# Handing over by token tile between the stages of a two-block network on one core

## The reference, cut to what matters

```python
# first block, layers i = 0, 1
h  = h + mixers(rms_norm(h, g_mix[i]) @ w_in[i]) @ w_out[i]
hn = rms_norm(h, g_ffn[i])
h  = h + (swiglu(hn) if i == 0 else moe_swiglu(hn))     # 8 experts, each token takes 2
gate = sigmoid(rms_norm(h, g_ple[i]) @ ple_gate_w[i])
h  = h + (p[i] @ ple_proj_w[i]) * gate                   # the "embedding part"
x  = rms_norm(h, g_final)
# second block, layers l = 0, 1; sh, sc, g come from silu(c) @ ada_w[l] + ada_b[l]
x = x + g1 * (mixers2((rmsnorm(x, g) * (1 + sc1) + sh1) @ w_in[l]) @ w_out[l])
x = x + g2 * swiglu(rmsnorm(x, g) * (1 + sc2) + sh2)
return rmsnorm(x, final_g)
```

## Time and profile before

| | |
|---|---|
| time of 3 runs, median (lowest to highest) | 2287.8 us (2281.92 to 2294.17) |
| the profiled execution: its time | 2287.38 us |
| its span from first to last instruction | 2286.0 us |
| PE busy | 2176.0 us, 95% of the span |
| DVE busy, ACT busy | 696.2 us (30%), 421.6 us (18%) |
| mean granted clock of TensorE | 0.974 of full |
| read from memory | 520.39 MB |

### The profile page before, as it was taken

One profiled execution on the slowest core, in us unless ns is written; L12 is line 12 of the kernel. 1 busy time (PEld: TensorE's weight loads), 2 busy tenths in 40 slices (PEclk: granted clock), 3 DMA queues, 4 the chain that ended last, 5 costly groups with the idle time before them and its releaser, 6 DMA issues.

```text
span 2286.0 us, 28880 instructions
## 1 busy us (share of the span) xinstructions
PE 2176.0 (95%) x12233; PEld 1270.5 (56%) x12233; DVE 696.2 (30%) x1453; ACT 421.6 (18%) x952; POOL 0.2 (0%) x4
## 2 busy tenths in 40 slices
PE   8988999989979999999999999889999999989998
PEld 5664777765755533333323232365677776657775
DVE  2563375223662100100111001125436533730001
ACT  2464000022462000000000000132310002320001
POOL 0000000000000000000000000000000000000000
PEclk9998999999979999999999999999999999999999
DMA  5222987023301999899999999422199532247400
GB/s 220 89 100 87 423 324 285 26 99 131 109 32 74 426 409 391 331 375 425 393 419 403 396 425 393 171 79 106 56 402 373 218 150 82 76 166 303 152 24 19
DMA packets 55143, 523.38 MB, mean 229 GB/s; under 512 B 6368, under 2 KB 6880, under 8 KB 16864
## 3 DMA queue, kind: packets, MB, share of 16 engines
q1 hardware_dynamic: 45792, 471.13, 51.0%
q10 hardware_dynamic: 9216, 50.34, 5.9%
HBM read 520.39 MB, written 1.05 MB: 228 GB/s over the span
## 4 chain that ended last, share of the span: by engine, by line
PE 87%; DVE 7%; ACT 4%; issue 1%; DMA 1%; DVEq 0%; SPq 0%; ACTq 0%
PE ps L89 87%; DVE ring L89 5%; ACT ring L89 2%; DVE stat L89 1%; DVE natural L89 1%; DVE residual L89 0%; ACT transposed L89 0%; ACT L89 0%; DMA ring<-in_moe 0%; DVE transposed L89 0%; DMA constants<-in_const 0%; ACT natural L89 0%; ACT stat L89 0%; DVE gates L89 0%; ACT z L89 0%
## 5 line engine op out<-in xcount | busy, mean ns | idle before, releaser
L89 PE MATMUL ps<-ring 128*32 128x512 f32 (+10 forms) x3812 | 536.6, 515 | 10.0 <-ACT ring L89 3.7
L89 PE MATMUL ps<-ring,transposed 128*128 128x384 f32 (+4 forms) x1408 | 475.7, 495 | 3.6 <-ACT transposed L89 3.5
L89 PE MATMUL ps<-ring,z 128*32 128x512 f32 (+3 forms) x2048 | 475.8, 584 | 0.3 <-ACT z L89 0.3
L89 PE MATMUL ps<-transposed,ring 128*128 128x256 f32 x2112 | 468.0, 380 | 5.6 <-issue 2.3
L89 PEld LDWEIGHTS ps<-transposed,ring 128*128 128x128 f32 x2112 | 402.2, 191 | 86.5 <-issue 31.2
L89 PEld LDWEIGHTS ps<-ring,transposed 128*128 128x128 f32 x1408 | 263.9, 193 | 191.4 <-issue 65.1
L89 PEld LDWEIGHTS ps<-ring 128*32 128x32 f32 (+4 forms) x3812 | 199.2, 129 | 291.2 <-issue 264.8
L89 DVE TENSOR_TENSOR z<-z,ps 128x256 f32<-128x256 f32 (+3 forms) x138 | 57.5, 417 | 924.2 <-ACT z L89 895.0
L89 PEld LDWEIGHTS ps<-ring,z 128*32 128x32 f32 (+2 forms) x2048 | 174.4, 139 | 249.1 <-issue 243.6
L89 ACT ACTIVATE z<-ps 128x256 f32<-128x256 f32 (+2 forms) x143 | 54.9, 384 | 938.7 <-PE ps L89 938.7
L89 ACT COPY z<-ps 128x256 f32<-128x256 f32 (+6 forms) x154 | 63.4, 412 | 632.0 <-PE ps L89 630.7
(11 more groups left out here) (123 smaller groups left out, 905.6 us busy)
## 6 DMA issues: line engine op xcount, KB each, us to landing
ring<-in_moe SPq DMA_DIRECT2D x88, 2048.0 KB, 13.6
ring<-in_ffn SPq DMA_DIRECT2D x66, 1536.0 KB, 13.2
ring<-in_moe SPq DMA_DIRECT2D x88, 1024.0 KB, 12.3
ring<-in_w_in SPq DMA_DIRECT2D x26, 1536.0 KB, 6.4
z<-in_ada ACTq DMA_DIRECT2D x48, 768.0 KB, 6.1
ring<-in_w_out SPq DMA_DIRECT2D x12, 1536.0 KB, 6.6
natural<-in_ada ACTq DMA_DIRECT2D x16, 768.0 KB, 6.7
ring<-in_ple_gate SPq DMA_DIRECT2D x4, 1536.0 KB, 6.6
```

The source lines that it names most:

```text
L89: self.ins = None if self.book.counting else op(*args, **kw)
```

## The change

Each helper that worked on both tiles now takes the tile `i`, and the engines' orders are written out by tile. What it does, part by part:
- Feed-forward: the down products of the last four blocks (18 to 21) are formed for tile 0 first, and those of tile 1 after all of tile 0's. Where a stage follows (`after`), the turn of tile 0 stands ahead of the last block's down products of tile 1. The hidden buffers are four instead of two, and silu and product share one.
- `ple0` and `ple1`: the six steps go tile by tile. Their squares for the next norm stand between the sigmoids, with the Sqrt and Sigmoid tables loaded in turn. The turn of the next stage's tile 0 stands ahead of the last step (`mix1`) or just behind it (`mixb0`); the first projection of tile 0 goes ahead of the turn of tile 1.
- `mixb1`: PE goes from `ffnb0` to the first projection of tile 0, then adapt, then the turn of tile 1. `mixb0`: turn of tile 0, adapt, first projection of tile 0, turn of tile 1.
- Ends of the mixers: DVE norms tile 0 before the last adds of tile 1.
- The scaled tile is signalled in halves (`xt{i}{q}`), and first products wait for the half they read.
- `ple0`'s weights lie in slots 7 (embedding) and 4, 5, 6 (gates), `ple1`'s gates in 1, 8, 9. The transfers of `mix1` no longer wait for `ple0`.
- The output is stored in four pieces of 256 KB instead of two of 512 KB.
- `everywhere()` now stands first in the program and `gathered()` last, next to the rest.

```diff
-    PLE_UP_SLOT, PLE1_UP_SLOT, PLEG = 0, 8, [[1, 2, 3], [1, 2, 5]]
+    PLE_UP_SLOT, PLE1_UP_SLOT, PLEG = 7, 8, [[4, 5, 6], [1, 8, 9]]
...
     def pe_win(s, t, i, where, width, parts=(0, 1)):
...
         for part in parts:
+            if t == 0:
+                pe.wait_ge(f"{s}.xt{i}{part}")
...
-    ff_silu, ff_hid = fw(2, SEQ), fw(2, SEQ)
+    ff_hid = fw(4, SEQ)
...
     def act_ff_silu(s, j):
         act.wait_ge(f"{s}.up{j}")
-        if j > 1:
-            act.wait_ge(f"{s}.hid{j - 2}")
-        act(S.activation, ff_silu[:, j % 2, :], ps[:, j % 2, 0:SEQ], ACT.Silu).then_inc(f"{s}.silu{j}")
+        if j > 3:
+            act.wait_ge(f"{s}.down{j - 4}")
+        act(S.activation, ff_hid[:, j % 4, :], ps[:, j % 2, 0:SEQ], ACT.Silu).then_inc(f"{s}.silu{j}")
...
-    def pe_ff(s, ada):
-        pe.wait_ge(*xt_ready(s, 1))
+    def pe_ff(s, ada, after):
         pe_ff_up(s, 0, False)
         for j in range(FB):
             if j + 1 < FB:
                 pe_ff_up(s, j + 1, ada is not None and j + 1 == ADA_TOTAL)
-            pe_ff_down(s, j)
+            pe_ff_down(s, j, (0, 1) if j < FB - 4 else (0,))
+        for j in range(FB - 4, FB):
+            if j == FB - 1 and after is not None:
+                pe_turn_h(after, 0)
+            pe_ff_down(s, j, (1,))
...
     def ple_columns(n):
-        c, i = divmod(n, 2)
+        i, c = divmod(n, 3)
...
     def pe_mixers1(l):
-        pe_turn_h(s)
-        win(0, 0)
+        if l == 0:
+            pe_turn_h(s, 0)
+            pe_turn_h(s, 1)
+            win(0, 0)
+        else:
+            win(0, 0)
+            pe_turn_h(s, 1)
         win(0, 1)
...
-        dve_residual(s, f"ffn{l}", banks=BANKS1)
-        dve_norm(f"ffn{l}")
-        dve_scale_xt(f"ffn{l}", column(l, "g_ffn"))
+        for i in range(NT):
+            dve_residual(s, f"ffn{l}", i, banks=BANKS1)
+            dve_norm(f"ffn{l}", i)
+        for i in range(NT):
+            dve_scale_xt(f"ffn{l}", i, column(l, "g_ffn"))
...
     def pe_mixers2(l):
-        pe_adapt(l)
-        pe_turn_h(s)
-        win(0, 0)
+        if l == 0:
+            pe_turn_h(s, 0)
+            pe_adapt(l)
+            win(0, 0)
+        else:
+            win(0, 0)
+            pe_adapt(l)
+        pe_turn_h(s, 1)
         win(0, 1)
...
-        dve_residual(s, f"ffnb{l}", 0, BANKS2)
-        dve_norm(f"ffnb{l}")
+        dve_residual(s, f"ffnb{l}", 0, 0, BANKS2)
+        dve_residual(s, f"ffnb{l}", 1, 0, BANKS2, (0,))
+        dve_norm(f"ffnb{l}", 0)
+        dve_residual(s, f"ffnb{l}", 1, 0, BANKS2, (1,))
+        dve_norm(f"ffnb{l}", 1)
...
-        sp_mixers1(1, [("ple0.up5",), ("ple0.gate1",), ("ple0.gate3",), ("ple0.gate5",)])
+        sp_mixers1(1, after)
...
-        sp_mixers2(0, [("ple1.h11",), ("ple1.gate1",), ("ple1.gate3",), ("ple1.h11",)])
+        sp_mixers2(0, [("ple1.h11",), ("ple1.gate3",), ("ple1.h11",), ("ple1.h11",)])
...
     def pe_first():
         pe_mixers1(0)
-        pe_ff("ffn0", 0)
-        pe_turn_h("ple0")
-        pe_ple(0)
+        pe_ff("ffn0", 0, "ple0")
+        pe_ple(0, 0)
+        pe_turn_h("ple0", 1)
+        for n in range(1, 5):
+            pe_ple(0, n)
+        pe_turn_h("mix1", 0)
+        pe_ple(0, 5)
         pe_mixers1(1)
...
     def act_second():
+        act_root_table()
+        act_norm("ple1", 0)
+        act_norm("ple1", 1)
+        act_ple_table()
+        act_ple(1, 0)
+        act_ple(1, 1)
+        act_ple(1, 2)
+        for n in range(3):
+            act_ple_square(1, "final1", n)
+        act_ple(1, 3)
+        act_root_table()
+        act_mean_root("final1", 0, PLE_PARTS)
+        act_norm("mixb0", 0)
+        act_ple_table()
+        act_ple(1, 4)
+        act_ple_square(1, "final1", 3)
+        act_ple_square(1, "final1", 4)
+        act_ple(1, 5)
+        act_root_table()
+        act_ple_square(1, "final1", 5)
+        act_mean_root("final1", 1, PLE_PARTS)
+        act_modulate_xt("mixb0", 0, gains[:, 0:8], mod[:, 0:8])
+        act_norm("mixb0", 1)
...
     def dve_second():
...
+        for n in range(4):
+            dve_ple(1, n)
+        dve_final("final1", 0, PLE_PARTS, h, "mixb0.h")
+        dve_norm("mixb0", 0)
+        dve_ple(1, 4)
+        dve_ple(1, 5)
+        dve_modulate_xt("mixb0", 0, gains[:, 0:8], mod[:, 0:8])
+        dve_final("final1", 1, PLE_PARTS, h, "mixb0.h")
+        dve_norm("mixb0", 1)
...
+        dve_residual("ffnb1", "final2", 0, 1)
+        dve_final("final2", 0, HALVES, xn, "final2.out")
+        dve_residual("ffnb1", "final2", 1, 1)
+        dve_final("final2", 1, HALVES, xn, "final2.out")
...
-            with nc.If(most <= P):
+            with nc.If(most > P):
+                everywhere()
+            with nc.Else():
                 gathered()
-                apart()
-            with nc.Else():
-                everywhere()
```

More of the change, by code:

```diff
@@ L336, in dve_sums, with dve_norm, dve_diagonal @@
         dve(V.tensor_scalar, sums[:, 0:1], sums[:, 0:1], 1e-6, None, ALU.add).then_inc(f"{s}.sum{i}")
[L338 to L343, removed]
+    def dve_norm(s, i, parts=HALVES):
+        dve_sums(s, i, parts)
+        dve_diagonal(s, i)
+    def dve_diagonal(s, i):
+        dve.part("norm")
+        dve.wait_ge(f"{s}.root{i}")
+        dve(V.reciprocal, stat[:, i:i + 1], stat[:, i:i + 1])
+        dve(V.tensor_scalar, diag[:, i, :], C("ident"), stat[:, i:i + 1], None, ALU.mult).then_inc(f"{s}.diag{i}")
     def dve_natural(s):
@@ L381, in act_modulate_xt @@
+    def act_modulate_xt(s, i, mult, add):
         act.part("turn")
         act.wait_ge(f"{s}.modulation")
[L383 to L392, removed]
+        act.wait_ge(f"{s}.turned{i}1")
+        for n in range(4, KD):
+            act(S.activation, xt[:, n, i * P:(i + 1) * P], ps[:, 2 * i + 1, (n - 4) * P:(n - 3) * P], ACT.Identity,
+                bias=add[:, n:n + 1], scale=mult[:, n:n + 1])
+        act.then_inc(f"{s}.xt{i}1")
@@ L1428, in act_ada_load @@
         if n == 0:
[L1429 removed]
+            act.wait_ge(f"{s}.xt10", f"{s}.xt11")
         if n > 1:
@@ L2092, in act_ple @@
-    def act_ple(l):
+        c, i, at, width = ple_columns(n)
+        w = slot(PLEG[l][c])[:, 0:KD * width].rearrange("p (k n) -> p k n", k=KD)
+        if i == 0:
+            pe.wait_ge(f"{s}.gate_w{c}")
+        if n > 1:
+            pe.wait_ge(f"{s}.mul{n - 2}")
+        for k in range(KD):
+            if c == 0 and k % 4 == 0:
+                pe.wait_ge(f"{s}.xt{i}{k // 4}")
+            mm(ps[:, 4 + n % 2, 0:width], xt[:, k, i * P:(i + 1) * P], w[:, k, :], k == 0, k == KD - 1)
+        pe.then_inc(f"{s}.gate{n}")
@@ L2093, in act_ple, with act_ple_table @@
+        if l == 0:
+            if n < 2:
+                pe.wait_ge(f"{s}.up_w", f"ple0.h1{n}")
+            for k in range(2):
+                mm(ps[:, 6 + n % 2, 0:width], pl_pT[:, k, i * P:(i + 1) * P], slot(PLE_UP_SLOT)[:, k * D + at:k * D + at + width],
+                   k == 0, k == 1)
+            pe.then_inc(f"{s}.up{n}")
+    def act_ple_table():
+        act(S.activation, stat[:, 14:15], stat[:, 13:14], ACT.Sigmoid)
+    def act_ple(l, n):
         s = f"ple{l}"
         act.part("ple")
[L2095 to L2100, removed]
@@ L2711, in act_mixers1 @@
         if l == 0:
-            act_squares(s, HALVES, "x{i}")
-        else:
-            act_squares(s, PLE_PARTS, "ple0.add{n}")
+            act.part("norm")
+            act_root_table()
+            for i in range(NT):
+                act_norm(s, i, "x{i}")
         z(0, 0)
@@ L2791, in act_mixers1 @@
         act_at_out(l, 1)
-        act_squares(f"ffn{l}")
+        act.part("norm")
+        act_root_table()
+        for i in range(NT):
+            act_norm(f"ffn{l}", i)
     def dve_mixers1(l):
@@ L3011, in act_mixers2 @@
         act_copy_mixed2(l, "re")
-        act_squares(f"ffnb{l}")
-        act_modulate_xt(f"ffnb{l}", gains[:, 8:16], mod[:, 24:32])
+        act.part("norm")
+        act_root_table()
+        for i in range(NT):
+            act_norm(f"ffnb{l}", i)
+        for i in range(NT):
+            act_modulate_xt(f"ffnb{l}", i, gains[:, 8:16], mod[:, 24:32])
     def dve_mixers2(l):
@@ L3126, in pe_second @@
     def pe_second():
-        pe.wait_ge("ple1.h11")
-        pe_turn_h("ple1")
-        pe_ple(1)
-        for l in range(2):
-            pe_mixers2(l)
-            pe_ff(f"ffnb{l}", 1 if l == 0 else None)
+        pe_turn_h("ple1", 0)
+        pe_turn_h("ple1", 1)
+        for n in range(6):
+            pe_ple(1, n)
+        pe_mixers2(0)
+        pe_ff("ffnb0", 1, "mixb1")
+        pe_mixers2(1)
+        pe_ff("ffnb1", None, None)
     def act_first():
```

299 lines of the change are left out of this document (170 added, 129 removed).

## The result

| | before | after |
|---|---|---|
| median of 4 runs (lowest to highest) | 2285.11 us (2281.92 to 2294.17) | 2261.43 us (2260.70 to 2263.78) |
| the profiled execution | 2287.38 us | 2261.43 us |
| its span, mean granted clock | 2286.0 us, 0.974 | 2260.1 us, 0.980 |

The ratio is 0.990, with a 95% interval of 0.9884 to 0.9911. The forecast was 2264 us, 2254 to 2276. The kernel is faster by 1.03%, and 2264 was 2.6 us too slow.

The account below looks back on a forecast made before the run. PE, busy for 95% of the span, was taken as the bound, leaving its pauses and half clock around changes of stage to gain; the terms sum to 23.8 us off the profiled 2287.4, so 2264 us, range 2254 to 2276.

Parts of the forecast that it names:

- ple0 to mix1: Change of stage from ple0 to mix1: projection and last step cover both tiles' chains; gain 5.7 us, bounds 3.5 and 5.8.
- order of the MoE versions, entry: Jump now ahead of `gathered()`, hidden under PE's 2.80 us wait for expert weights: 0, bounds 0 and a loss of 2.4.
- MoE to ple1: End of the MoE: without the jump's stall, PE starts behind the second turn; gain 3.3 us, bounds 1.5 and 4.8.
- ple1 to mixb0: Largest term: tile 0's norms and diagonal run beside ple1's steps 4 and 5; gain 8.3 us, bounds 4 and 9.4.
- mixb0 to ffnb0: Start of ffnb0's up products: tile 0 turns 1.7 us earlier, tile 1's diagonal 0.6; gain 1.05 us, bounds 0.5 and 2.7.
- ffnb0 to mixb1: Tile 0's chain runs beside tile 1's down products, only tile 1's modulation remains; gain 1.1 us, bounds 0 and 2.2.
- the end: ffnb1 to the end: DVE is the bound, tile 1's work stays behind tile 0's final products; gain 0.9 us, bounds 0 and 1.5.
- The late weights of ple0: Before ple0's first step: gate weights queued behind embedding weights; wait of 3.0 us, then 1.7 us for half clock.
- Rival 2: Before ple0: weights are in time, so the loss of 2.3 becomes a gain of 2.4; 2259 us, chance 0.09.
- Three of the forecast's signs: MoE's first product still waits for weights; no new PE wait above 2 us elsewhere; diagonal waits fall from 32.9 to under 10.
- Rival 1: Changes of stage: half clock at up to three more places, a late ple1 chain, uncovered jump; gain 12.4, 2275 us, chance 0.20.
- Rivals 3 and 4: 3: feed-forward buffer waits stall PE each block, 2300 us, chance 0.03; 4: PE still stops at each change, 2282, chance 0.05.

## Why the prediction was right

All in us; gains are positive. Those measured are differences of the two profiled executions by the prediction's own marks.

| change of stage | predicted | measured |
|---|---|---|
| mix0 to ffn0 | 2.25 | 2.2 |
| ffn0 to ple0 to mix1 | -2.3 + 5.7 = 3.4 | 3.9 |
| mix1 to the router | 1.5 | 1.4 |
| order of the MoE versions, entry | 0 (0 to -2.4) | -3.8 |
| MoE to ple1 | 3.3 | 4.7 |
| ple1 to mixb0 | 8.3 | 8.1 |
| mixb0 to ffnb0, ffnb0 to mixb1 | 2.15 | 3.3 |
| mixb1 to ffnb1 | 2.0 | 2.3 |
| the end | 0.9 | 3.2 |
| sum | 23.8 | 25.3 |

The two profiles differ by 25.9 us; 0.5 of the rest is mix0's own variation. The medians differ by 23.7, since the profiled execution of before lay 2.3 us above its median. That the forecast of 23.8 fits the medians to 0.1 is therefore luck, and that its sum fits the profiles to 1.5 us is in part luck too: the MoE gave 2.4 us less than foretold, and other places 3.9 more.

*The steps that held.* The long chains were priced from the old rows and came out to within 0.3 us each: ple0 to mix1 5.6 us for 5.7, mixb0 to ffnb0 0.9 for 1.05, ffnb0 to mixb1 0.8 for 1.1. Behind ple1 nothing is left but the modulation (0.95 us against 1.15 foretold), and undoing that place alone costs 7.2 us. The late weights of ple0 were the one loss that I foretold inside the change: a wait of 3.0 and 1.7 of half clock, measured 2.24 and 1.80 (a loss of 1.7 us in place of 2.3). Taking the transfer order away took both away, so the cause is shown. Rival 2, weights in time, failed, as its bytes said.

*The step that failed: the jump.* I let "2.2 to 2.4 us of jump fit in" under a wait of 2.80 us. The price of a jump had been read at the end of the MoE, where it was 2.2 to 2.4 us, and was taken to a place where the weight stream fills the transfer engines; there it is 5.5 to 6.2 us. PE's pause grew by 2.7 us and brought about 1 us of half clock: 3.8, beyond my bound of 2.4. The run with the loads held back separates the two halves. At the MoE's own end I had 3.3, with 1.1 charged for a clock that stayed up and 0.4 for a short branch, and 4.7 came. So the swap is a draw, as the run without it shows. Three of the forecast's signs did not come out: the MoE's first product no longer waited for its weights, a new wait above 2 us stood at the entry, and the waits on diagonals stayed at 15.7 us.

*The term mis-sized: the end.* I reckoned that tile 1's work stays behind tile 0's final products, and gave 0.9. But three more pairs of tile 1's down products now stand behind tile 0's last (3 x 1.71 = 5.1 us). DVE's first add of tile 0 began 7.68 us ahead of the end of the last product instead of 2.54. Tile 0 was finished, its output included, before tile 1's first bank was ready, and DVE stood 0.96 us waiting for that bank. The first row is of before, the others of after:

```profile
2272.61 0.69 DVE L89 TENSOR_TENSOR natural<-ps,gates 128x512 f32<-128x512 f32 x1 [3.46 <-PE ps L89]
```

```profile
2244.91 0.69 DVE L89 TENSOR_TENSOR natural<-ps,gates 128x512 f32<-128x512 f32 x1 [1.74 <-PE ps L89]
...
2251.77 0.69 DVE L89 TENSOR_TENSOR natural<-ps,gates 128x512 f32<-128x512 f32 x1 [0.96 <-PE ps L89]
```

I had DVE as the bound at the end and didn't ask what lets it start. Measured 3.2, and 4.3 by the run that takes the order away. Of the whole miss of 1.5 us in the sum, this is +2.3, the MoE -2.4 and the rest +1.6, about what full clock at the start of ffnb0 gave.

*The clock.* I charged half clock to one pause of 3.0 us, half to one of 2.6, and left ffnb0's open. It did not come: the pause there fell from 2.12 to 1.75 us, and ffnb0's first 64 instructions of up products took 14.05 us instead of 15.71. My basis was misread in one place: I had half clock behind both pauses of the earlier trace rows, but behind the second, of 2.35 us, the granted clock was 1.00 (2047.4 to 2048.5 us of before). What ran at 0.50 there were the first turns (2040 to 2042 us), behind a pause of 2.62. Rival 1's further half clock came at one place, the entry, not three, and none of its late chains came. Its uncovered jump was right as a mechanism and priced too low. Rivals 3 and 4 are refuted, the one by the run with the buffers alone, the other by the table.

## What to carry to other kernels

When both tiles' norms stand between two stages, give the first tile's chain the last products of the second to hide under, and price the place by the chain from last product to diagonal against those products; here that was good to 0.3 us. Then look at what the reordering does to the transfer queue: slots come free in another order, and one early but unneeded load ahead of the first needed one cost 4 us. A taken branch over a long program has no fixed price: measure it where it will stand, with the transfers that run there.

## What the runs showed of the hardware

- A jump over the long version cost ACT and DVE 2.1 to 2.6 us at the MoE's end, 3.2 to 3.3 at its entry with the loads held back, and 5.7 to 6.2 beside a transfer share of 0.99.
- A pause of 2.24 to 2.39 us before ple0 was followed by half clock in all six profiles with that order of transfers (7.11 or 7.12 us for the step), one of 2.54 before ple1 was not (clock 1.00). With 12 products whose outcome nobody reads in the pause, the step behind it ran at full clock (5.43 us).
- The first mixers took 3 us more or less with the same code. In 120 to 150 us PE's granted clock was 0.89 in the four profiles of the changed kernel and its variants in which ffn0 began at 226.3 to 227.4 us, and 0.79 or 0.80 in the five in which it began at 229.0 to 229.7. What puts a run into one group or the other stays open.
- An ACT table load takes 1.28 us, and the next activation follows 0.02 us later. Four more of them cost no time that shows: ple1 took PE 27.71 us before and after. The Trainium skill (ScalarE: Activation LUTs, "What ACT_TABLE_LOAD costs") has 2.66 us for a switch, with a drain. By my estimate from that figure the ple1 term would have been 3 us less than the 8.3 foretold; 8.1 was measured, so the page's figure does not hold here.
